# Gated DeltaNet on one core: odd heads run one chunk behind even heads, in 64x64 tile products

## What is computed

```python
def step(state, inp):
    q_i, k_i, u_i, w_i, a_i, g_i = inp
    v_new = u_i - jnp.einsum('bhck,bhkv->bhcv', w_i, state)
    o = (jnp.einsum('bhck,bhkv->bhcv', q_i * jnp.exp(g_i)[..., None], state)
         + jnp.einsum('bhcs,bhsv->bhcv', a_i, v_new))
    g_last = g_i[..., -1]
    state = (state * jnp.exp(g_last)[..., None, None]
             + jnp.einsum('bhck,bhcv->bhkv', k_i * jnp.exp(g_last[..., None] - g_i)[..., None], v_new))
    return state, o
```

## Time and profile before

| | |
|---|---|
| median of 3 runs | 1890.22 us (1889.98 to 1891.20) |
| the profiled execution, own time | 1890.07 us |
| its span in the profile | 1888.3 us |
| PE / DVE / ACT / POOL busy | 98% / 48% / 24% / 55% |
| granted TensorE clock | 0.999 |

### The profile page before, as it was taken

How to read it: one execution, slowest core, us unless ns; L and a number is a source line. 1 busy time by engine, 2 the same in 40 slices (tenths; PEclk the granted TensorE clock), 3 DMA queues, 4 the chain that set the end, 5 groups by cost and what they waited for, 6 DMA issues and landing times.

```text
span 1888.3 us, 26079 instructions
## 1 busy us (share of the span) xinstructions
PE 1858.6 (98%) x9980; PEld 1511.8 (80%) x9980; DVE 898.5 (48%) x1375; ACT 448.9 (24%) x788; POOL 1032.4 (55%) x580
## 2 busy tenths in 40 slices
PE   7999999999999999999999999999999999999998
PEld 6887788668888888888888778886788888888887
DVE  6687545664354323223266855466535542314141
ACT  6333213441113000000154233153501220000010
POOL 5543166326566666666654523662356666667662
PEclk9999999999999999999999999999999999999999
DMA  6222023113233323333342211330222323333322
GB/s 221 81 62 68 23 90 101 56 31 127 90 91 113 96 93 101 95 95 101 100 135 68 68 57 35 100 101 28 86 90 90 100 90 100 100 94 96 100 91 76
DMA packets 46759, 167.06 MB, mean 88 GB/s; under 512 B 5018, under 2 KB 8346, under 8 KB 46146
## 3 DMA queue, kind: packets, MB, share of 16 engines
q1 hardware_dynamic: 44066, 154.30, 26.3%
q10 hardware_dynamic: 2592, 11.29, 1.6%
HBM read 159.28 MB, written 6.29 MB: 88 GB/s over the span
## 4 chain that ended last, share of the span: by engine, by line
PE 90%; DVE 7%; issue 1%; ACT 1%; DMA 0%; POOL 0%; SPq 0%; ACTq 0%; DVEq 0%; POOLq 0%
PE ps L420 26%; PE ps L422 25%; PE ps L421 25%; PE ps L832 2%; PE ps L854 1%; DVE lanes L1582 1%; PE ps L842 1%; PE ps L638 1%; PE ps L645 1%; PE ps L669 1%; DVE ps L1598 1%; PE ps L494 1%; DVE outer L1595 1%; DVE acc L1371 1%; DVE negmax L1787 1%
## 5 line engine op out<-in xcount | busy, mean ns | idle before, releaser
L395 POOL TENSOR_SCALAR wHi<-wraw 128x1024 fp32r<-128x1024 f32 x288 | 308.2, 1070 | 803.8 <-PE ps L422 790.2
L397 POOL TENSOR_TENSOR wLo<-wraw,wHi 128x1024 fp32r<-128x1024 f32 x288 | 724.2, 2515 | 24.0
L420 PE MATMUL ps<-hHi,wHi 128*128 128x512 f32 x1376 | 554.1, 403 | 4.6 <-POOL wLo L397 2.6
L422 PE MATMUL ps<-hHi,wLo 128*128 128x512 f32 x1376 | 537.2, 390 | 0.0
L421 PE MATMUL ps<-hLo,wHi 128*128 128x512 f32 x1376 | 536.9, 390 | 0.0
L420 PEld LDWEIGHTS ps<-hHi,wHi 128*128 128x128 f32 x1376 | 259.1, 188 | 68.8 <-issue 11.4
L422 PEld LDWEIGHTS ps<-hHi,wLo 128*128 128x128 f32 x1376 | 258.7, 188 | 55.3
L421 PEld LDWEIGHTS ps<-hLo,wHi 128*128 128x128 f32 x1376 | 259.2, 188 | 49.5 <-issue 1.4
L420 PE MATMUL ps<-fHi,wHi 128*128 128x512 f32 x640 | 249.3, 389 | 0.0
L422 PE MATMUL ps<-fHi,wLo 128*128 128x512 f32 x640 | 249.0, 389 | 0.0
L421 PE MATMUL ps<-fLo,wHi 128*128 128x512 f32 x640 | 249.0, 389 | 0.0
(11 more groups left out here) (289 smaller groups left out, 2030.0 us busy)
## 6 DMA issues: line engine op xcount, KB each, us to landing
wraw<-stream SPq DMA_DIRECT2D x288, 512.0 KB, 3.5
out<-xT ACTq DMA_DIRECT2D x2, 2048.0 KB, 8.2
xT<-out ACTq DMA_DIRECT2D x2, 2048.0 KB, 9.0
xin<-x SPq DMA_DIRECT2D x4, 512.0 KB, 6.0
out<-ost ACTq DMA_DIRECT2D x1, 1024.0 KB, 4.2
out<-ost ACTq DMA_DIRECT2D x2, 512.0 KB, 3.8
prm<-params ACTq DMA_DIRECT2D x1, 647.0 KB, 4.0
prm<-params SPq DMA_DIRECT2D x1, 576.0 KB
```

The costliest lines, as they stand in the source:

```text
L395: nc.gpsimd.tensor_scalar(wHi[:, slot], wraw[:, raw], 1.0, 0.0, ALU.mult, ALU.add).then_inc(unit_high, 1)
L397: nc.gpsimd.tensor_tensor(wLo[:, slot], wraw[:, raw], wHi[:, slot].bitcast(F32), ALU.subtract).then_inc(unit_split, 1)
L420: mm(o, lh[lc], rh[rc], start=start, stop=False)
L422: return mm(o, ll[lc], rh[rc], start=False, stop=stop)
```

## The change

`chains(step)` gives, for steps 0 to 8, the pairs (parity of head, chunk): even heads work on chunk `step`, odd heads on chunk `step - 1`. The two chunks lie on different halves of the partitions. Every product of the recurrence becomes a 64x64 one, and even and odd heads alternate. Key part, query part, inverse product, state update and output product are five groups of up to eight such products; the old 128x128 products fall away, the zero halves of `vnew` and the zero blocks of `state` too. Each group of a step writes one PSUM bank for both parities.

Per step one projection step is left, after the key products (`av 1`, steps 0 to 7). `turn_delta_output(0)` stands there in step 8. The query products stand behind the inverse products, the output products of the same step behind the state update; a new semaphore `query_done` orders the last two. `av 2` is projected whole behind the loop. In `lower_products` and `corner_products` four groups become two, in which the halves `ch` alternate. Four projection steps follow each group of the lower products; of the corner products, four stand before the first group and four between the two.

ACT loads the table for Sqrt before the loop, copies `vnew` for both parities in one instruction (128x256) and the output in two (64x256 each). DVE makes `r` in up to two instructions of 64x256, `sdec` and the new state in one of 128x256 each; `av 1` is taken behind the loop.

The diff, its new lines (the lines taken out are those of the functions above):

```diff
+def chains(step):
+
+    return [(par, step - par) for par in range(2) if 0 <= step - par < CHUNKS]
...
+FRONT, BACK = 1920, 288
...
+    query_done = 8; ws_done = 8; r_ready = 8; tr_done = 9; vnew_done = 9; supd_done = 8; sdec_done = 7; state_done = 8; o_done = 9; o_copied = 9

...
+        eglb, expa = sb("eglb", [P, PAIRS, CHUNKS + 1]), sb("expa", [HEADS, 1])
...
+        r, vnew = at(56, "r", [P, PAIRS, 64]), at(58, "vnew", [P, 2, PAIRS, 64])
+        state, sdec = at(88, "state", [P, PAIRS, 64]), at(90, "sdec", [P, PAIRS, 64])
...
+                    for hf in range(2):
                         for n in range(16):
                             g = 16 * hf + n
                             tt, h = divmod(g, HEADS)
...
+                            for ch in range(2):
+                                last = mm(S(2 + 2 * hf + ch)[64 * ch + 32:64 * ch + 64, 32 * n:32 * n + 32],
+                                          gated[64 * ch:64 * ch + 32, tt, 0, h, 32:64], upper[64 * ch:64 * ch + 32, g], start=True, stop=True)
+                        last.then_inc(lower_done, 2)
+                        project(("z", 3), range(4 * hf, 4 * hf + 4))

                 def corner_products():

                     pe.wait_ge(inv_placed, layer * per.inv_placed + 3)
                     pe.wait_ge(lower_copied, layer * per.lower_copied + 4)
...
+                    project(("av", 0), range(0, 4))
+                    for hf in range(2):
                         for n in range(16):
                             g = 16 * hf + n
                             tt, h = divmod(g, HEADS)
...
+                            for ch in range(2):
+                                last = mm(S((4 + 2 * hf + ch) % 6)[64 * ch:64 * ch + 32, 32 * n:32 * n + 32],
+                                          lower[64 * ch + 32:64 * ch + 64, g], gated[64 * ch + 32:64 * ch + 64, tt, 0, h, 32:64], start=True, stop=True)
+                        last.then_inc(corner_done, 2)
+                        if hf == 0:
+                            project(("av", 0), range(4, KD))
+
+                def recur(step):
+
+                    both = chains(step)
+                    hs = lambda m: np.s_[64 * (m % 2):64 * (m % 2) + 64]
+                    cs = lambda par: np.s_[64 * par:64 * par + 64]
+                    if step == 0:
+                        pe.wait_ge(corner_placed, layer * per.corner_placed + 2)
                     else:
...
+                        pe.wait_ge(state_done, layer * per.state_done + step)
                         for j in range(PAIRS):
...
+                            for par, m in both:
+                                if m:
+                                    last = mm(S(2)[hs(m), j * 64:j * 64 + 64], kqe[cs(par), j, m // 2, m % 2, 0], state[cs(par), j], start=True, stop=True)
                         last.then_inc(ws_done, 1)
...
+                        if step < CHUNKS:
+                            project(("av", 1), range(step, step + 1))
+                        else:
+                            turn_delta_output(0)
+                        pe.wait_ge(r_ready, layer * per.r_ready + step)
+                    for j in range(PAIRS):
+                        for par, m in both:
+                            h = 2 * j + par
+                            last = mm(S(2)[hs(m), 256 + j * 64:256 + j * 64 + 64], gated[hs(m), m // 2, 0, h],
+                                      r[hs(m), j] if m else rhsv[hs(m), 0, h * 64:h * 64 + 64], start=True, stop=True)
                     last.then_inc(tr_done, 1)
...
+                    if step == 0:
+                        project(("av", 1), range(0, 1))
+                    if step == 1:
+                        pe.wait_ge(corner_placed, layer * per.corner_placed + 4)
+                    if step >= 2:
+                        pe.wait_ge(o_copied, layer * per.o_copied + step - 1)
+                    for j in range(PAIRS):
+                        for par, m in both:
+                            if m:
+                                last = mm(S(step % 2)[hs(m), j * 64:j * 64 + 64], kqe[cs(par), j, m // 2, m % 2, 1], state[cs(par), j],
+                                          start=j == 0, stop=False, skip_group_check=True)
+                    if step:
+                        last.then_inc(query_done, 1)
+                    pe.wait_ge(vnew_done, layer * per.vnew_done + step + 1)
+                    if step < CHUNKS:
+                        for j in range(PAIRS):
+                            for par, m in both:
+                                if m < CHUNKS - 1:
+                                    h = 2 * j + par
+                                    last = mm(S(3)[cs(par), j * 64:j * 64 + 64], kend[hs(m), m // 2, h * 64:h * 64 + 64], vnew[hs(m), step % 2, j],
+                                              start=True, stop=True)
+                        last.then_inc(supd_done, 1)
+                    if step == 0:
+                        pe.wait_ge(corner_placed, layer * per.corner_placed + 4)
                     else:
...
+                        pe.wait_ge(query_done, layer * per.query_done + step)
+                    chunk_output(step)
+
+                def chunk_output(step):
+
+                    for j in range(PAIRS):
+                        for par, m in chains(step):
+                            hs = np.s_[64 * (m % 2):64 * (m % 2) + 64]
+                            last = mm(S(step % 2)[hs, j * 64:j * 64 + 64], gated[hs, m // 2, 1, 2 * j + par], vnew[hs, step % 2, j],
+                                      start=m == 0 and j == 0, stop=j == PAIRS - 1, skip_group_check=True)
                     last.then_inc(o_done, 1)

...
+                for step in range(CHUNKS + 1):
+                    recur(step)
                 turn_delta_output(1)
+                project(("av", 2))
...
+                    act.wait_ge(o_copied, layer * per.o_copied + 2 * tt + 3)
...
+                def copy_output(step):
+                    act.wait_ge(o_done, layer * per.o_done + step + 1)
+                    for par, m in chains(step):
+                        rows = np.s_[64 * (m % 2):64 * (m % 2) + 64]
+                        ins = nc.scalar.copy(o_tm[rows, m // 2].rearrange("p (j q v) -> p j q v", j=PAIRS, q=2)[:, :, par],
+                                             S(step % 2)[rows, 0:256].rearrange("p (j v) -> p j v", j=PAIRS))
+                    ins.then_inc(o_copied, 1)
+                    if step and step % 2 == 0:
+                        square_o(step // 2 - 1)
+
+                nc.scalar.preload_act_table(ACT.Sqrt)
+                for step in range(CHUNKS + 1):
+                    rows = np.s_[0:64] if step == 0 else np.s_[64:128] if step == CHUNKS else np.s_[0:128]
+                    act.wait_ge(tr_done, layer * per.tr_done + step + 1)
+                    nc.scalar.copy(vnew[rows, step % 2].rearrange("p j v -> p (j v)"), S(2)[rows, 256:512]).then_inc(vnew_done, 1)
+                    if step in (4, 6, 8):
+                        root_o((step - 4) // 2)
+                    copy_output(step)
...
+                nc.vector.memset(state[64:128], 0.0).then_inc(vector_step, 1)
+                dve.wait_ge(vector_step, steps.next())
...
+                by_pair = lambda t: t.rearrange("p (j v) -> p j v", j=PAIRS)
+                for step in range(CHUNKS + 1):
+                    if step:
+                        dve.wait_ge(ws_done, layer * per.ws_done + step)
+                        for par, m in chains(step):
+                            if m:
+                                hs = np.s_[64 * (m % 2):64 * (m % 2) + 64]
+                                ins = tt_(r[hs], rhsv[hs, m // 2].rearrange("p (j q v) -> p j q v", j=PAIRS, q=2)[:, :, par],
+                                          by_pair(S(2)[hs, 0:256]), ALU.subtract)
+                        ins.then_inc(r_ready, 1)
+                    if 0 < step < CHUNKS:
+                        dve.wait_ge(state_done, layer * per.state_done + step)
+                        tt_(sdec[:], state[:], eglb[:, :, step:step + 1].broadcast_to([P, PAIRS, 64]), ALU.mult).then_inc(sdec_done, 1)
+                    if step in (3, 5, 7):
+                        sum_o((step - 3) // 2)
+                    if step in (6, 8):
+                        scale_o((step - 6) // 2)
+                    if step == CHUNKS:
                         gate_o(0)
...
+                    else:
+                        dve.wait_ge(supd_done, layer * per.supd_done + step + 1)
+                        if step:
+                            rows = np.s_[64:128] if step == CHUNKS - 1 else np.s_[0:128]
+                            dve.wait_ge(sdec_done, layer * per.sdec_done + step)
+                            tt_(state[rows], sdec[rows], by_pair(S(3)[rows, 0:256]), ALU.add).then_inc(state_done, 1)
+                        else:
+                            nc.vector.tensor_copy(state[0:64], by_pair(S(3)[0:64, 0:256])).then_inc(state_done, 1)
```

(27 more changed lines are left out.)

66 lines of the change are left out of this document (1 added, 65 removed).

## The result

The changed kernel takes 1876.48 us, median of 4 runs (1875.48 to 1877.79); the kernel before took 1890.71 beside it. The ratio is 0.9917, 95% interval 0.9903 to 0.9930. The forecast was 1871, with a range of 1866 to 1883. The profiled execution took 1875.96 us with a span of 1873.2.

A forecast was written before the change was run, and what follows sets the result against it. PE's own list and the short waits in it were taken to bound the kernel. Gains of 5.5 (lower and corner products) and 4.1 us (recurrence and ends) make 9.6 a layer, 19.2 off 1890.07: 1871 us, range 1866 to 1883.

The forecast's parts named there:

- The price of a group: Recurrence groups: 16 records of 64x64 products in different tiles overlap and take 0.46 us; without overlap 0.91.
- The lower and corner stretch: Lower and corner products before the loop: 16.2 us a layer instead of 21.65, a gain of 5.5.
- The start rate of records: Rival: records cannot start faster than 34 ns each, giving 1883 us; chance 0.16, shared with late ACT or DVE instructions.
- The ring: Waits between PE, DVE and ACT in a full step (steps 2 to 7): 4.0 us together.
- The ends: Steps 0, 1 and 8, turn of output 1 and av 2 around the full steps; whole stretch 40.9 us, before 44.98.
- the clock falls: Rival: PE's busy share in a step drops to some 78%, clock goes to 1.2 GHz, about 1904 us; chance 0.02.
- The shared bank: Rival: row tiles writing one bank wait for each other, recurrence groups take 0.91 us, 1895 us in all; chance 0.10.
- The table load for nothing: Rival: load before the last corner copies costs nothing, 1.28 us less a layer, 1868 us; within full overlap's 0.70.
- What lies behind the loop: Taking av 1 and av 2, gating and turned outputs after the loop: nothing waits, cost 0.

The follow-up runs named there:

- e4: Kernel before with only the new lower and corner products; 1881.93 us, ratio 0.9943 to the kernel before.
- e3: Changed kernel with the even heads' products first, then the odd heads', in all five recurrence groups; 1892.60 us, ratio 1.0010 to the kernel before.
- e1: Changed kernel with ACT's Sqrt table load moved between the two halves of the corner copies; 1872.36 us, ratio 0.9900 to the kernel before.
- e10: Changed kernel without the early table load line, so the load comes with the first root in step 4; 1874.70 us, ratio 0.9895 to the kernel before.
- e9: Changed kernel with even heads' products before odd heads' in each group and the table load between the corner copies' halves; 1882.91 us, ratio 0.9949 to the kernel before.
- e2: Changed kernel with two projection steps of av 2 moved from behind the loop into step 0; 1874.12 us, ratio 0.9898 to the kernel before.

## Why the prediction was right, and where it was not

**The price of a group** was right: with overlap, 0.46 us for 16 records. The trace has 0.52 from group to group, transition included, and groups of 64 in 1.20. The lower and corner stretch took 16.32 us (sum: 16.2), and e4 gives 5.2 of the 5.5 us. The start rate of records is no limit here: 34 ns a record would have made 2.2 us of a group of 64.

**The ring** was right: 4.0 us forecast, 3.99 measured; steps 2 to 7 take 218.31 - 194.37 = 23.94 us where the sum had 24.1. The idle times are where they were put, 0.23 us before the key products for one.

**The ends** are where the forecast failed, in the step "the load used to stand in step 4, beside other work. So the state update starts at T + 3.0 and step 1 at T + 4.2". The place and the size of the wait were right (1.46 us forecast as 1.6; step 1 at T + 4.4 and T + 4.3). What was missing is what the wait does to the clock. Step 1 was priced at full clock, 3.8 us, and took 5.86 and 5.09: 3.4 us in the two layers. The forecast was 5.1 us too low against the profiled execution (1870.9 against 1875.96), and the measured time lies in the range because that reached up to 1883 for another rival, the start rate; that part is luck. The rest of the miss is small: step 0 0.3 in the two layers together, step 8 0.2 each, and 1.0 us between span and own time (1875.96 - 1873.2 against 1890.07 - 1888.3). The rival "the clock falls" named the effect but put it in the wrong place: it looked at the busy share of a full step, and it had that too low (78%; the windows of full steps have PE busy for 3.52 to 3.88 of 3.99 us). Those steps run at the full clock in every kernel but e3, and there only behind the wait. It was the wait, in front of steps that without it keep the full clock.

**The shared bank** fell. In step 1 even and odd heads have different names in the trace, so that single records show. The timeline of PE in the changed kernel, at the low clock:

```profile
191.40 0.31 PE L652 MATMUL ps<-r,gated 64*64 64x64 f32 x1
191.41 0.31 PE L652 MATMUL ps<-rhsv,gated 64*64 64x64 f32 x1
191.51 0.31 PE L652 MATMUL ps<-r,gated 64*64 64x64 f32 x1
191.51 0.31 PE L652 MATMUL ps<-rhsv,gated 64*64 64x64 f32 x1
```

Both write the bank of `S(2)`, from different row halves, and a pair starts together every 0.11 us. The Trainium skill, "TensorEngine Tiling (Array Packing)", section "Gotcha 1: PSUM Pressure", says that different row tiles cannot access the same bank at the same time; in these runs they do, where the partitions they write differ, and at the full clock a group of 16 such records takes 0.52 us. Two row tiles on the same partitions of one bank were not tried.

**The table load for nothing** was named as a rival (1868 us) and is what e1 and e10 reach, by other means. By the length e1 stands 5.9 us under the changed kernel, at 1870; 2.6 of these are the load, the rest is the clock, which the rival had not priced. **What lies behind the loop** waited for nothing, as said: from the turn of output 1 to that of output 2 e1 and the changed kernel both take 7.3 us.

## What to carry to other kernels

A wait is not priced by its length alone: 1.46 us of PE idle time in place of 0.17 cost 1.3 us of delay and another 1.2 to 2.1 of low clock behind it, and two projection steps as filler saved the second part though the delay stayed. When two gains are put together, look at the seam: here each part alone kept the clock, and only both together uncovered a table load. Small products pay by their place in the list: with neighbours in different tiles of the array a group of 16 takes 0.52 us, where 16 in one tile took 0.91; in two runs, one tile after the other, two groups took 1.43 in e9 (193.79 to 195.22), 0.72 each.

## What the runs showed of the hardware

- **Records start out of order between tiles, but only a few ahead.** In the changed kernel, step 3, query products (L664) begin while six of the sixteen records of the inverse products (L652) in front of them have yet to start:

```profile
200.00 0.51 PE L652 MATMUL ps<-r,gated 64*64 64x64 f32 x10
200.29 0.27 PE L664 MATMUL ps<-state,kqe 64*64 64x64 f32 x2
200.34 0.28 PE L652 MATMUL ps<-r,gated 64*64 64x64 f32 x3
```

  In odd steps the two groups lie in different tiles, in even steps (the step at 196.00) in the same ones, and there they do not cross. The Trainium skill, "TensorE: Matmul & The Clock Gate", section "Part 3: Packing small matmuls — row/col tiling", has matmuls start strictly in program order; between different tiles the trace shows otherwise. In e9 the same look ahead makes a group of two runs 0.96 us long, where 16 records in one tile last 1.14: in its step 1, whose records have different names, the odd heads' records start at 189.28, while those of the even heads go on to 189.45.
- **Issue is faster than the densest row had shown.** 64 records of 32x32 in 1.20 us are 19 ns a record, where L552 had 34.
- **The clock fell for another wait too.** In e2's trace, as in the five others with the wait near 48 us, PE idles for 4.1 us, and the window that begins in this wait has the low clock. Windows of e2:

```profile
40.00:48.50 8.50, 6.87 (x37) 5.78 (x36) 8.22 (x11) 2.96 (x5) 5.42 (x4) 1.00 0.38 124
48.50:55.30 6.80, 4.33 (x13) 3.49 (x14) 5.98 (x7) 1.09 (x2) 1.35 (x1) 0.50 0.21 77
```

- **DVE's part in that wait goes with POOL's.** PE waits there for `xrow`; L1543, the last but one DVE instruction on it, takes 2.76 us in e2 and 0.67 in e1. First DVE and POOL in e2, then DVE in e1:

```profile
47.63 2.76 DVE L1543 SCALAR_TENSOR_TENSOR xrow<-xrow,arow 40x512 f32<-40x512 f32 x1
...
47.51 2.35 POOL L402 TENSOR_TENSOR wLo<-wraw,wHi 128x1024 fp32r<-128x1024 f32 x1
...
44.98 0.67 DVE L1543 SCALAR_TENSOR_TENSOR xrow<-xrow,arow 40x512 f32<-40x512 f32 x1
```

  In all six traces with the wait, POOL's split (the line that makes `wLo`) starts 0.1 to 0.2 us before this instruction, which then takes 2.74 to 2.77 us; in the six without it POOL does nothing at that time, and it takes 0.67. No run moved one of the two, so this is what the traces have in common, not a cause that was tried, and why POOL is earlier or DVE later in some executions stays open.
